# One Trainium2 core, hybrid attention layer: late modulation groups moved from the head to the mixer, early modulation mixed of split and unsplit chunks, last down group in token halves

## What is computed

```python
cs = silu(c)                                   # two rows: c of the prompt, c of the sample
mod = cs @ w_mod + b_mod                       # 2048 x 12288: shift, scale, gate of both parts
h = rmsnorm(x, g_attn) * (1 + sc_a) + sh_a
z = h @ w_in                                   # 2048 x 4608
oa = rmsnorm(diff_attention(...), subln_g) * (1 - lambda_init)
ob = sliding-window attention with sinks
x = x + gt_a * (concat(oa, ob) @ w_out)        # 2048 x 2048
h2 = rmsnorm(x, g_ffn) * (1 + sc_f) + sh_f
u = h2 @ w_up                                  # 2048 x 11264
y = conv_b + sum of conv_w[j] * shifted u      # causal, width 3
x = x + gt_f * ((silu(gate) * val) @ w_down)   # 5632 x 2048
return rmsnorm(x, g_final)                     # and the new keys, values, conv state
```

## Time and profile before

| | us |
|---|---|
| median of 3 runs | 2709.91 (2707.13 to 2711.16) |
| the profiled execution | 2706.82 |
| its span, first to last instruction | 2705.0 |
| PE busy | 2619.0 (97%) |
| DVE busy | 1634.6 (60%) |
| ACT busy | 958.4 (35%) |
| POOL busy | 524.9 (19%) |

### The profile page before, as it was taken

The page is one execution under the profiler, slowest core; times in us unless marked ns, Lnnn a source line. Parts: engine busy times, 40 slices in busy tenths (PEclk is TensorE's granted clock), DMA queues, the critical chain, the costliest instruction groups (busy, mean ns, idle before and its releaser), DMA issues.

```text
span 2705.0 us, 50278 instructions
## 1 busy us (share of the span) xinstructions
PE 2619.0 (97%) x19783; PEld 2448.8 (91%) x19783; DVE 1634.6 (60%) x3210; ACT 958.4 (35%) x1871; POOL 524.9 (19%) x461
## 2 busy tenths in 40 slices
PE   7999999999999999999999999999999999999997
PEld 2268889898988999899999999999999999999997
DVE  1469889874357888965554555555455555445554
ACT  2236666664344335422222222222222222222224
POOL 1057777761003452400000000000000000000003
PEclk9999999999999999999999999999999999999998
DMA  8886556562215654432332332233232223223231
GB/s 256 265 266 192 172 181 182 171 161 60 59 48 160 172 164 125 148 110 81 92 94 84 90 93 80 80 94 94 79 94 83 82 88 94 87 86 94 79 94 70
DMA packets 416210, 324.96 MB, mean 120 GB/s; under 512 B 44410, under 2 KB 360218, under 8 KB 414880
## 3 DMA queue, kind: packets, MB, share of 16 engines
q1 hardware_dynamic: 410032, 302.55, 37.6%
q0 software_dynamic: 5248, 14.56, 1.7%
q10 hardware_dynamic: 688, 4.47, 0.5%
HBM read 307.67 MB, written 14.07 MB: 119 GB/s over the span
## 4 chain that ended last, share of the span: by engine, by line
PE 84%; DVE 7%; DMA 3%; issue 2%; POOL 2%; ACT 1%; SPq 1%; ACTq 0%; DVEq 0%; POOLq 0%
PE ps L1584 25%; PE ps L1586 24%; PE ps L1585 24%; PE ps L1558 4%; DVE late_f L1256 3%; PE ps L1673 2%; PE ps L1639 2%; DMA w_raw<-in_w_out 2%; DMA w_raw<-in_w_mod 1%; PE ps L1657 1%; POOL oT L708 1%; DVE w_lo L1149 1%; SPq L547 1%; ACT w_hi L806 1%; PE ps L1595 1%
## 5 line engine op out<-in xcount | busy, mean ns | idle before, releaser
L1584 PE MATMUL ps<-x_hi,w_hi 128*128 128x272 f32 (+1 forms) x4480 | 1320.1, 295 | 32.1 <-DVE w_lo L1149 22.5
L1585 PE MATMUL ps<-x_lo,w_hi 128*128 128x272 f32 (+1 forms) x4480 | 1298.2, 290 | 0.0
L1586 PE MATMUL ps<-x_hi,w_lo 128*128 128x272 f32 (+1 forms) x4480 | 1296.2, 289 | 0.0
L1584 PEld LDWEIGHTS ps<-x_hi,w_hi 128*128 128x128 f32 x4480 | 850.3, 190 | 45.9 <-issue 27.6
L1586 PEld LDWEIGHTS ps<-x_hi,w_lo 128*128 128x128 f32 x4480 | 852.0, 190 | 0.0
L1585 PEld LDWEIGHTS ps<-x_lo,w_hi 128*128 128x128 f32 x4480 | 849.8, 190 | 0.0
L806 ACT ACTIVATE w_hi<-w_raw 128x1024 fp32r<-128x1024 f32 x368 | 375.0, 1052 | 1049.6 <-PE ps L1586 901.5
L1149 DVE TENSOR_TENSOR w_lo<-w_raw,w_hi 128x1024 fp32r<-128x1024 f32 x368 | 456.6, 1270 | 343.1 <-ACT w_hi L806 342.7
L1586 PE MATMUL ps<-y_hi,w_lo 128*128 128x272 f32 x1408 | 406.8, 289 | 0.0
L1584 PE MATMUL ps<-y_hi,w_hi 128*128 128x272 f32 x1408 | 406.1, 288 | 0.0
L1585 PE MATMUL ps<-y_lo,w_hi 128*128 128x272 f32 x1408 | 404.5, 287 | 0.0
(11 more groups left out here) (195 smaller groups left out, 2095.8 us busy)
## 6 DMA issues: line engine op xcount, KB each, us to landing
w_raw<-in_w_mod SPq DMA_DIRECT2D x192, 512.0 KB, 4.6
w_raw<-in_w_up SPq DMA_DIRECT2D x176, 512.0 KB, 4.6
w_raw<-in_w_down SPq DMA_DIRECT2D x88, 512.0 KB, 4.2
w_raw<-in_w_in SPq DMA_DIRECT2D x56, 512.0 KB, 3.9
w_raw<-in_w_in SPq DMA_DIRECT2D x32, 256.0 KB, 3.7
w_raw<-in_w_out SPq DMA_DIRECT2D x16, 512.0 KB, 5.3
w_raw<-in_w_out SPq DMA_DIRECT2D x64, 128.0 KB, 3.9
x_transposed<-xT SPq DMA_DIRECT2D x4, 1088.0 KB, 8.6
```

The source lines that it names most:

```text
L1584: pe.matmul(out[:, 0:n], hi_w, hi_x, start=first, stop=False)
L1585: pe.matmul(out[:, 0:n], hi_w, lo_x, start=False, stop=False)
L1586: return pe.matmul(out[:, 0:n], lo_w, hi_x, start=False, stop=last)
```

## The change

**Late groups.** Eleven groups in the mixer, four in the output stretch, one in the head. The mixer's chunks stay in half slabs 2 to 49, 88 of them in place of 80. The head's four hidden tiles have 1, 2, 3 and 2 late chunks in place of 3, 4, 5 and 4.

**Early modulation.** 27 of the 64 chunks, the odd ones from 7 to 59 (`SPLIT`), are split as all other weights are: ACT makes the high part and DVE the low part, three chunks ahead (`AHEAD`), and PE multiplies each of them by `c_parts`, the high and low parts of cs (four columns), in fp32r. The other chunks stay in fp32, with `c_whole`, cs and two columns of zeros. The rows have four lines, and `group_columns` adds them in pairs by a matmul with `pair`. A slot with a split chunk is free after the low part. ACT and DVE now run a loop over e in which each piece of work has its place: the split first, then group_out or group_mod, x, the norm, and hT, x_hi, x_lo by a table (`H_AT`).

**Last down group.** It is made in token halves: sixteen column tiles for tokens 0 to 271, then the same sixteen for 272 to 543, with chunks 4 to 7 of its weights in other buffers (`tail_w`). The final norm runs on tokens 0 to 255 and 256 to 543 (`FINAL`) apart; the first half's rows are finished and stored during the second half.

```diff
+SPLIT = range(7, 60, 2)
+ES = len(SPLIT)
+AHEAD = 3
+H_AT = {SUM_AT + 3: 0, SUM_AT + 4: 2, 36: 4, 37: 6, 52: 8, 53: 10}
-LATE1 = 10 * LPG
+LATE1 = 11 * LPG
 LATE2 = 4 * LPG
-LATE3 = 2 * LPG
+LATE3 = LPG
-for _first, _then in ((0, 3), (1, 3), (1, 4), (4, 0)):
+for _first, _then in ((0, 1), (1, 1), (1, 2), (2, 0)):
...
 @@ sync: slot_free
                 if old[0] == "w":
-                    sp.wait_ge(s_lo, old[1] + 1)
+                    sp.wait_ge(s_lo, ES + old[1] + 1)
+                elif old[0] == "e" and old[1] in SPLIT:
+                    sp.wait_ge(s_lo, SPLIT.index(old[1]) + 1)
                 elif old[0] == "e":
                     sp.wait_ge(m_used, old[1] + 1)
...
 @@ sync: the stores of y
-            for t, ready, n in ((0, f_scd, 1), (2, f_sca, 1), (1, f_scd, 2), (3, f_sca, 2)):
+            for t, ready, n in ((0, f_scd, 1), (1, f_sca, 1), (2, f_scd, 2), (3, f_sca, 2)):
...
 @@ scalar, early
+            for e in range(EC):
+                if e + AHEAD in SPLIT:
+                    hi_split(e + AHEAD)
+                if e % EPG == 1 and e > EPG:
+                    group_out(e // EPG - 1)
+                if 0 <= e - X_AT < KT:
+                    x_in(e - X_AT)
+                if e == X_AT + 1:
                     act.wait_ge(lam_dot, 2)
                     act.activation(tiny[:, 4:6], tiny[:, 6:8], ACT.Exp).then_inc(lam_exp, 1)
...
+                if e == SUM_AT + 1:
+                    root(0, n0_rstd[:, :])
+                if e in H_AT:
+                    h_hi(H_AT[e])
+                    h_hi(H_AT[e] + 1)
             hi_early(0)
             hi_early(1)
-            group_out(7)
+            group_out(E_GROUPS - 1)
...
 @@ vector, early
+            for e in range(EC):
+                if e + AHEAD in SPLIT:
+                    lo_split(e + AHEAD)
+                if e == 6:
+                    dve.wait_ge(rows_t, len(ROW_COUNTS))
+                    for i in range(1, len(ROW_COUNTS)):
+                        row_out(i)
...
+                if 1 <= e - X_AT < KT:
+                    sum_row(e - X_AT)
+                if e % EPG == 2 and e > EPG:
+                    group_mod(e // EPG - 1)
+                if e == SUM_AT + 2:
...
+                    dve.wait_ge(sd_ok, 1)
+                    dve.reciprocal(n0_rstd[:, :], n0_rstd[:, :]).then_inc(rs_ok, 1)
...
+            lo(0, RAW_OF[("w", 0)] % NR, ES)
+            lo(1, RAW_OF[("w", 1)] % NR, ES + 1)
+            group_mod(E_GROUPS - 1)
+            dve.wait_ge(mod_ok, KT // EGT)
+            for kt in range(3 * EGT, KT):
+                h_mul(kt)
+            for kt in range(3 * EGT, KT):
+                h_lo(kt)
...
 @@ tensor, early
+                    if e in SPLIT:
+                        n = SPLIT.index(e) % NW
+                        pe.matmul(bank(7 - g % 2)[0:4, :], c_parts[:, kt, :], w_hi[n][:, EG * k:EG * k + EG],
+                                  start=kt == 0, stop=False)
+                        mm = pe.matmul(bank(7 - g % 2)[0:4, :], c_parts[:, kt, :], w_lo[n][:, EG * k:EG * k + EG],
+                                       start=False, stop=kt == KT - 1)
+                    else:
+                        mm = pe.matmul(bank(7 - g % 2)[0:4, :], c_whole[:, kt, :], w_raw[raw][:, EG * k:EG * k + EG],
+                                       start=kt == 0, stop=kt == KT - 1)
...
 @@ tensor, tail
-            for n in range(8):
-                down(GRP * (NG - 1) + n // 2, (LAST_DOWN + 2 * (n // 2), None), (NG - 1) % 2,
-                     range(4 * (n % 2), 4 * (n % 2) + 4))
-                if n:
-                    y_turn(range(2 * n - 2, 2 * n))
-            y_turn(range(KT - 2, KT))
...
+            for h in range(2):
+                for n in range(KT):
+                    down_last(h, n)
+                    if n % 2 and n > 1:
+                        y_turn(h, n - 3)
+                        y_turn(h, n - 2)
+                    if h and n == 1:
+                        y_turn(0, KT - 2)
+                        y_turn(0, KT - 1)
+                    if h and n == 3:
+                        token_sums(0)
+                    if h and n == 7:
+                        pe.wait_ge(c_val, FT)
+                        for r in range(4):
+                            mm = pe.transpose(bank(3)[0:2 * FT, P * r:P * r + P], u_last[:, :, r], ident[:, :])
+                        mm.then_inc(uc_t, 1)
+            y_turn(1, KT - 2)
+            y_turn(1, KT - 1)
+            token_sums(1)
```

More of the change, by code:

```diff
@@ L419, in build, with tail_w, last_bank @@
         st3.close()
-        f_sq, f_sum = cv, ext[1][:, 0:T]
+        f_sq, f_sum, xg = cv, ext[1][:, 0:T], [ext[0][:, 0:T], n2_rstd]
+        FINAL = ((0, 2 * P), (2 * P, T - 2 * P))
+        FINAL_TILES = ((0, 1), (2, 3, QT))
+        def tail_w(c):
+            if c < NW:
+                return w_hi[c][:, :], w_lo[c][:, :]
+            if c < NW + 2:
+                at = slice(CW * (c - NW), CW * (c - NW) + CW)
+                return [b[1][:, :, :].rearrange("p k n -> p (k n)")[:, at] for b in (y_hi, y_lo)]
+            flat = x_lo[:, :, :].rearrange("p k n -> p (k n)")
+            first = 2 * CW + 2 * CW * (c - NW - 2)
+            return flat[:, first:first + CW], flat[:, first + CW:first + 2 * CW]
+        def last_bank(i):
+            return bank(4 + i % 4)
         ps = ctx.enter_context(nc.psum_tensor("ps", [P, 8, 512], F32))
@@ L825, in group_out, with hi_split, x_in @@
                     act.wait_ge(e_t, g - 1)
-                act.activation(mod_rows[g % 2][:, :], bank(7 - g % 2)[0:2, :], ACT.Copy).then_inc(e_ev, 1)
-            for kt in range(KT):
-                if (X_AT + kt) % EPG == 0:
-                    group_out((X_AT + kt) // EPG - 1)
+                act.activation(mod_rows[g % 2][:, :], bank(7 - g % 2)[0:4, :], ACT.Copy).then_inc(e_ev, 1)
+            def hi_split(e):
+                n = SPLIT.index(e)
+                if n >= NW:
+                    act.wait_ge(m_used, SPLIT[n - NW] + 1)
+                hi(n, RAW_OF[("e", e)] % NR, LOADED[("e", e)])
+            def x_in(kt):
                 act.wait_ge(xt_t, kt + 1)
@@ L1519, in _ @@
+            final_scale(1)
         @block.tensor
@@ L1822, in _, with down_last @@
[L1822 to L1826 removed]
+            def down_last(h, n):
+                i, nn = KT * h + n, n % 2
+                if h == 0 and nn == 0:
+                    lo_ready((LAST_DOWN + n // 2, None))
+                pe.wait_ge(d_ev, DOWN0 + i + 1)
+                a, c = HALF[h]
+                hi_w, lo_w = tail_w(n // 2)
+                for kt in range(GRP):
+                    w = slice(256 * kt + P * nn, 256 * kt + P * nn + P)
+                    mm = products(last_bank(i), c, hi_w[:, w], lo_w[:, w], y_hi[0][:, kt, a:a + c],
+                                  y_lo[0][:, kt, a:a + c], kt == 0, kt == GRP - 1)
+                mm.then_inc(d_done, 1)
```

326 lines of the change are left out of this document (177 added, 149 removed).

## The result

The changed kernel takes 2729.32 us (median; 2726.0 to 2735.2, one disturbed run left out) against 2709.91 before: a ratio of 1.0075, 95% interval 1.0058 to 1.0092. It is slower by 0.75%. I had predicted 2708.5, with a range up to 2725.

A forecast was written before the change was run, and what follows sets the result against it. PE was taken as full in the loop (1393 of 1400 us). Early 24.7, mixer 2.5, head -21.8, tail -6.8 sum to -1.4 against 2706.82: 2705.4; the median being 3.1 above, 2708.5 us, range 2692 to 2725.

The forecast's parts named there:

- Chunk 8: Early stretch: DVE's row copies stand behind low parts of split chunks, so chunk 8 starts 4.0 us later.
- Chunks 9 to 27: Early stretch: ten split chunks save 0.8 us each, waits for group_out cost 6.6; in all -1.7 us.
- First norm: Early stretch, chunk 28's end to group 3's columns: reciprocal behind lo(33), 20.1 us against 11.7, so +8.4.
- Chunks 34 to 63: Early stretch after the first norm: slots 1 and 3 turn in 7.1 us; 66.7 us against 57.7, so +9.
- Start of the projection: End of early stretch: tiles 10 and 11 done earlier, last hT no longer mixed with x_lo; -3 us.
- Clock: Early stretch: five new waits lower PE's clock, 1.7 us lost behind each; +8 us, between 0 and +17.
- Rival 2: Clock stays low through chunks 34 to 63, each burst short and followed by a wait: +18, time 2727; chance 10%.
- Mixer: 170 to 600 us: eight more late chunks raise DVE from 89% to 93%; +2.5 us, 0 to +19.
- Head: 1050 to 1200 us: eight late chunks leave, taking 22.2 us off DVE; -21.8 us, -16 to -23.
- Tail: Kernel's end: last product 1.3 later, way to scaling 2.1 shorter, stores 6.0 shorter; -6.8 us, -5 to -8.5.
- The loop: From 1200 us on: PE busy 1393 of 1400 us, the change leaves it alone; no term in the sum.
- early stretch: Up to the first projection product: terms from chunk 8 to clock sum to 24.7 us, between +14 and +34.

The follow-up runs named there:

- f2: Changed kernel with row copies, group_out and the first norm's reciprocal put ahead of split work on ACT and DVE: 2710.52 us, 1.001 of the kernel before.
- g4: Changed kernel in f2's order, with seven chunks split (35, 39 and so on to 59) in place of 27: 2693.75 us, 0.9946 of before.
- h1: Changed kernel with 86 small unused matmuls put where PE waited longest in the early stretch: 2716.26 us, 1.0035 of the kernel before.
- i2: e4 with ten late groups in the mixer and the last group not made at all: 2679.28 us, 0.9888 of the kernel before.
- e4: Kernel before with late groups moved and the tail changed, early stretch as before: 2686.45 us, 0.9909 of before.
- e2: Kernel before with the late groups alone moved: 2696.49 us, 0.9942 of before.
- e3: Kernel before with only the last down group in token halves and the final norm by FINAL halves: 2701.37 us, 0.997 of before.
- h2: Kernel before with 22 tiny matmuls at PE's start, putting the loop where the changed kernel has it: 2720.95 us, 1.0054 of before.
- e1: Kernel before with the early part of the change alone: 2755.84 us, 1.0168 of before.
- f1: Changed kernel with 16 tiny matmuls at PE's very start: 2717.14 us, 1.0035 of the kernel before.
- h3: Changed kernel in f2's order, with eleven chunks split (7, 9 and so on to 27) in place of 27: 2682.95 us, 0.9912 of before.
- f4: Changed kernel with no chunk split, all else as it is: 2688.41 us, 0.9925 of the kernel before.
- f3: Changed kernel with eight small unused matmuls behind each early chunk from 8 on: 2787.06 us, 1.029 of the kernel before.

## Why the prediction was wrong, step by step

**Chunk 8** (+4.0): measured 4.5 to 4.6. Right. **Chunks 9 to 27** (-1.7, where ten times 0.78 against 6.6 give -1.2): +4.6. The chunk behind the first stall ran at half clock (3.58 us in place of 1.8), one load took 7.34 us, and the waits for group_out were as named. f2, with three pieces of work in another place, had chunk 28 earlier than before, so the order cost this.

**First norm** (+8.4): +10. I had the low part of chunk 33 ahead of the reciprocal, but not the root and its table load (1.28), which ACT does behind the high part of chunk 31.

**Chunks 34 to 63** (+9): +17.5 (75.2 against 57.7), and +18.1 up to the first product: the largest miss. The waits were not what was too small. The forecast 66.7 had 24.2 of them, and PE waited 16.3. Its work took 58.9 and not 42.5: group columns are 1.05 us each for 0.4 (`pair`, and twice the matmuls), and most of the rest is half clock, which I had in a term of its own. "Slots 1 and 3 turn round in 7.1 us" was right from issue to low part (7.2), but it took each load as issued when its slot is free; seven of thirteen came behind the load of an unsplit chunk, which waits for PE, so that what slows PE slows the loads too. Each block of hT and x_lo kept PE waiting 3.6 us, 4 forecast. f2, in the best order, still lost 20 us between the first norm and the mixer, and g4 paid for each split chunk.

**Start of the projection** (-3): -1.7. **Clock** (+8): the pieces above are measured with the half clock in them. PE's busy time has some 17 us of it more than before had, and the chain of waits at most some 15; what it cost of the span is not shown, as told at h1. The mechanism, half clock behind the waits, is there, and 8 for it is less than half of the busy time that it took. I took 1.7 lost behind each wait; the two waits of 3.6 were followed by 9 us at half clock each (134.0 to 143.0 and 171.6 to 180.6, clock 0.50), 4.5 lost. Rival 2 did not come as such: over chunks 34 to 63 the clock was 0.82, not 0.5.

**Mixer** (+2.5): about 10. The term was mis-sized: I asked which vector engine gets full, and put PE's own sums and their waits at nothing ("Late tiles only move: no cost"). By i2 and e4, PE is busy 5.4 us longer there and idle 6.2 longer; why it is idle stays open. DVE was where I had it (399.2 of 430).

**Head** (-21.8): -25.6, in e2, e4 and after alike. All waits for w_lo went and the clock came back; the sums that I let move for nothing are part of the difference. **Tail** (-6.8): -8.4 in the profile, -9.8 as a median in e3. The last product was 1.8 later (1.3), the way to the scaling 3.8 (4.2), the store 6.5 (6.7).

**The loop** ("the change leaves the loop alone"): this is the step that failed outright. Its instructions are the same, but they stand some 90 further on in PE's program, and that costs 8 to 15 us in four returns (h2 8.2, the changed kernel 9.7, e1 15.3 against before). Without the second pause the changed kernel takes 2717 us (f1), inside my range; without the loop the terms of the profile after still sum to +12.7 where I had -1.4: early stretch, and mixer with output stretch, cost 11 and 9 more than forecast, head and tail gave 4 and 2 more.

## What to carry to other kernels

Before a chunk gets more steps between its load and the slot's release, compare the slot's turn (issue, landing, each step, each handover, and what else stands in those engines' queues) with what the matmul engine needs for as many chunks as there are slots, and look which load stands ahead of it in the queue and what that one waits for. Here the split gained in the profile where the second was longer, while x was transposed (h3), and not where PE was full with the chunks alone (g4). When an experiment makes a part thin, check in the trace that the part lies where the time is lost. When the order of a helper engine is rewritten, look first for the few instructions that everybody waits for, here the row copies, group_out and the reciprocal: f2 won 19 us by moving three of them. And after any edit ahead of a long loop, count the pauses at its return: a few instructions more or less, in a place where they cost nothing, were worth about 10 us in the loop here.

The best that was run is late groups and tail without the early part (e4, 0.9909 of before, and again 0.9914), or with eleven chunks split while x is transposed (h3, 0.9912).

## What the runs showed of the hardware that was not expected

At a loop's return PE pauses for some 1.7 us beyond its queue, and a second time for as long, some 3 us further on, in kernels whose loop stands at certain places of its program. With 15957, 16021, 16028, 16032 and 16111 instructions recorded on PE ahead of the loop's first product (before, f4, g4, h3, f1) there was one pause, with 16044 and 16048 (h2; after, f2 and e1) there were two. The numbers in the expectations are counted in another way and are some 35 lower. h1, 344 behind the changed kernel, has one, and f3, 1792 behind, two. Sixteen matmuls added at the program's start took 12 us off the kernel, 9.7 of them in the loop.

The granted clock fell to 0.50 behind waits of 3.6 us and more, and this hid a saving: the split took 21 us of full-clock work off PE in the early stretch, and PE was busy 145.7 us there, before 143.5.
